# Two transformer blocks in one launch: TensorE's ticks crossed where two stages open, and norms, low parts and means of squares reordered in differential attention's last turns

## The reference

```python
for i in range(2):
    h = rms_norm(x, attn_norm[i])              # x * rsqrt(mean(x*x) + eps) * gain
    mix = stick_breaking_mixer(h, w_in[0], w_out[0]) if i == 0 else diff_mixer(h, ...)
    x = x + mix
    x = x + swiglu_ffn(rms_norm(x, ffn_norm[i]), w_gate[i], w_up[i], w_down[i])

# diff_mixer, 8 heads, two maps each:
a = softmax(q1 @ k1.T * scale, masked) - lam * softmax(q2 @ k2.T * scale, masked)
o = a @ v
o = rms_norm(o, sub_g) * (1 - lam_init)        # per head
return o @ w_out
# swiglu_ffn:
return (silu(h @ w_gate) * (h @ w_up)) @ w_down
```

## Time and profile before

| what | us |
|---|---|
| median of 3 runs | 2243.19 (2242.12 to 2243.57) |
| the profiled execution | 2241.81 |
| its span, first to last instruction | 2240.1 |
| TensorE busy in it | 2209.8 (99%) |
| VectorE, ScalarE, GpSimd busy | 1201.5, 935.8, 219.7 |

### The profile page before, as it was taken

One profiled execution on the slowest core, in us unless ns is written; L12 is line 12 of the kernel. 1 busy time (PEld: TensorE's weight loads), 2 busy tenths in 40 slices (PEclk: granted clock), 3 DMA queues, 4 the chain that ended last, 5 costly groups with the idle time before them and its releaser, 6 DMA issues.

```text
span 2240.1 us, 26887 instructions
## 1 busy us (share of the span) xinstructions
PE 2209.8 (99%) x10484; PEld 1727.7 (77%) x10484; DVE 1201.5 (54%) x1827; ACT 935.8 (42%) x1561; POOL 219.7 (10%) x312
## 2 busy tenths in 40 slices
PE   8999999999999999999999999999999999999999
PEld 6768888678888888877565888888886657888887
DVE  4574564564444444564444555554546685555454
ACT  4464334554432322334545433333335564333332
POOL 0000221211200000121323100000210001000000
PEclk9999999999999999999999999999999999999999
DMA  5212112114222232222111233322222112323233
GB/s 174 78 54 89 44 35 84 50 48 137 96 96 94 94 104 94 95 86 75 38 48 38 85 102 97 103 94 95 94 95 66 54 41 75 104 94 96 93 99 108
DMA packets 52110, 187.48 MB, mean 84 GB/s; under 512 B 5904, under 2 KB 6032, under 8 KB 51856
## 3 DMA queue, kind: packets, MB, share of 16 engines
q1 hardware_dynamic: 51984, 185.76, 25.4%
HBM read 183.64 MB, written 2.10 MB: 83 GB/s over the span
## 4 chain that ended last, share of the span: by engine, by line
PE 93%; DVE 3%; ACT 3%; issue 1%; DMA 0%; SPq 0%; ACTq 0%; DVEq 0%
PE ps L936 22%; PE ps L939 22%; PE ps L942 22%; PE ps L960 4%; PE ps L963 4%; PE ps L961 4%; PE ps L923 2%; PE ps L1283 2%; PE ps L1134 1%; PE ps L1167 1%; PE ps L1023 1%; PE ps L1271 1%; PE ps L1259 1%; PE ps L1287 1%; PE ps L1047 1%
## 5 line engine op out<-in xcount | busy, mean ns | idle before, releaser
L1335 ACT CAST wh<-raw 128x1024 fp32r<-128x1024 f32 (+1 forms) x336 | 352.9, 1050 | 869.6 <-PE ps L942 783.2
L1669 DVE TENSOR_TENSOR wl<-raw,wh 128x1024 fp32r<-128x1024 f32 (+1 forms) x336 | 416.4, 1239 | 175.5 <-ACT wh L1335 174.5
L936 PE MATMUL ps<-hh,wh 128*128 128x512 f32 x1408 | 450.9, 401 | 13.3 <-ACT hh L1351 11.9
L939 PE MATMUL ps<-hh,wl 128*128 128x512 f32 x1408 | 436.0, 391 | 0.4 <-DVE wl L1669 0.4
L942 PE MATMUL ps<-hl,wh 128*128 128x512 f32 x1408 | 435.2, 390 | 0.6 <-DVE hl L1748 0.6
L936 PEld LDWEIGHTS ps<-hh,wh 128*128 128x128 f32 x1408 | 258.7, 189 | 69.7 <-ACT wh L1335 10.2
L942 PEld LDWEIGHTS ps<-hl,wh 128*128 128x128 f32 x1408 | 264.8, 188 | 57.4 <-DVE hl L1748 1.0
L939 PEld LDWEIGHTS ps<-hh,wl 128*128 128x128 f32 x1408 | 264.5, 188 | 57.7 <-DVE wl L1669 1.8
L936 PE MATMUL ps<-R,wh 128*128 128x512 f32 x896 | 287.0, 401 | 0.0
L939 PE MATMUL ps<-R,wl 128*128 128x512 f32 x896 | 277.5, 390 | 2.4 <-DVE wl L1669 2.4
L942 PE MATMUL ps<-R,wh 128*128 128x512 f32 x896 | 276.7, 389 | 0.0
(11 more groups left out here) (225 smaller groups left out, 2193.1 us busy)
## 6 DMA issues: line engine op xcount, KB each, us to landing
raw<-in_weights SPq DMA_DIRECT2D x332, 512.0 KB, 3.3
x<-in_x_t SPq DMA_DIRECT2D x4, 512.0 KB, 7.1
F<-in_x_t SPq DMA_DIRECT2D x4, 512.0 KB, 4.4
out<-x SPq DMA_DIRECT2D x8, 256.0 KB, 2.0
raw<-in_weights SPq DMA_DIRECT2D x4, 416.0 KB, 3.2
x<-in_bias SPq DMA_DIRECT2D x1, 1024.0 KB, 6.4
C<-in_consts SPq DMA_DIRECT2D x1, 832.0 KB, 6.4
F<-in_weights SPq DMA_DIRECT2D x2, 384.0 KB, 3.6
```

Of the source, the lines that this page charges most:

```text
L936: pe.matmul(out, hi[:, k, cs], B.tile(u.src, k)[0], start=k == 0, stop=False)
L939: pe.matmul(out, lo[:, k, cs], B.tile(u.src, k)[0], start=False, stop=False)
L1335: act.copy(B.wh[s][:, 0:nk * ncol], B.raw[s][:, 0:nk * ncol]).then_inc(S["w_hi"], 1)
L1669: dve.tensor_tensor(lo, src, hi.bitcast(F32), ALU.subtract).then_inc(S[name], 1)
```

## The change

Five edits to the order, none to what is computed; the counts of instructions are the same on each engine, and the queues of GpSimd and SyncE are unchanged word for word.

1. `dense(..., crossed=True)` in two stages, the opening of the second block (`uq[0] + uk[0]`) and the last feed-forward (`ff2b`): the first two ticks of unit 1 stand before the last tick of unit 0.
2. `diff`, group 0: `df_norm` stands before `df_soft` of its tick (heads 0 and 1 of the group, where both fall together).
3. The low part of a head (L1970) is made one tick later, except the last head's.
4. In the last turn the led products come one step earlier among the attention's ticks.
5. In `lead`, what a tick issues is put in another order: the low part of a chunk and the evictions come before the deferred steps (`hl`, squares).

```diff
                     first = self.split(units[0].chunks[0] + 2)
-                    rest = first + rest + self.ready(u, j)
-                if not (b == u.nk and j == 0):
-                    rest += self.low()
+                    rest = first + self.ready(u, j) + (self.low() if j else []) + rest
+                else:
+                    rest = self.low() + rest
...
-    def dense(self, units, more=None):
+    def dense(self, units, more=None, crossed=False):
...
+            order += [(u, piece) for piece in pieces]
+        if crossed:
+            order = order[:3] + order[4:6] + order[3:4] + order[6:]
+        for u, piece in order:
+            self.place(u)
...
             yield ([("df_soft", d, n - 1)] if d.g and 1 <= n < 17 else []) + [("df", d, n)]
-            if d.g == 0 and n < 16:
-                yield [("df_soft", d, n)]
             h = d.since(n, 1)
             if h is not None:
                 yield [("df_norm", d, h)]
+            if d.g == 0 and n < 16:
+                yield [("df_soft", d, n)]
...
-        self.run(self.dense(uq[0] + uk[0], roots(2, True)))
+        self.run(self.dense(uq[0] + uk[0], roots(2, True), True))
...
-        self.run(tail[:1] + made[:1] + tail[1:3] + made[1:2] + tail[3:4] + made[2:3] + tail[4:5] + made[3:5] + tail[5:] + made[5:])
+        self.run(made[:1] + tail[:1] + made[1:2] + tail[1:3] + made[2:3] + tail[3:4] + made[3:4] + tail[4:5] + made[4:6] + tail[5:] + made[6:])
...
-        self.run(self.dense(chain(ff2b), roots(5)))
+        self.run(self.dense(chain(ff2b), roots(5), True))
...
-        h = d.since(n, 3)
+        h = 3 if n == 22 else d.since(n - 1, 3)
```

More of the change, by code:

```diff
@@ L339, in heads @@
         self.defer(5, "dn_root", u)
-    def dense(self, units, more=None):
-        n = 0
+    def dense(self, units, more=None, crossed=False):
+        n, order = 0, []
         for u in units:
-            self.place(u)
             if u.kind == "rows":
@@ L349, in dense @@
                 pieces = [(i, a, a + 2) for i in range(4) for a in range(0, 8, 2)]
[L350 to L364, removed]
+            order += [(u, piece) for piece in pieces]
[3 more added lines that the diff above has]
+            self.place(u)
+            tick, extra = self.low() + self.due(), (more or {}).get(n, [])
+            n += 1
+            if u.kind == "rows" and piece[2] % u.nk == 0:
+                steps = self.ready(u, piece[2] // u.nk - 1)
+                tick += steps[:-1] + extra + steps[-1:]
+            else:
+                tick += extra
+            if u.kind == "cols" and piece[2] == 8:
+                if piece[0] == 3:
+                    tick.append(("ev", u))
+                    if u.ev == "dq":
+                        self.heads(u)
+                tick += self.split(u.chunks[piece[0]] + 2)
+            yield [("mm", u, *piece)], tick
         rest = self.due(True)
```

## The result

| what | before | after |
|---|---|---|
| median, us | 2242.23 (2241.75 to 2244.27, 20 runs) | 2247.38 (2242.34 to 2249.22, 20 runs) |
| ratio of the times, 95% interval | | 1.0018 (1.0012 to 1.0025) |
| the profiled execution, its span | 2241.81, 2240.1 | 2244.68, 2242.9 |

A forecast was written before the change was run, and what follows sets the result against it. TensorE, busy 2209.8 of 2240.1 us, was taken as the bound, so only waits could change. Crossings 1.8 + 3.35 less gains 4.65 gave +0.5 on 2243.19: 2243.7 us, range 2240.0 to 2247.5.

The forecast's parts named there:

- The crossing at the opening: Where the second block opens: TensorE waits for unit 1's low weights, cost 1.8 us, between 1.5 and 2.2.
- The norm first: First head of differential attention: norm ahead of the exponentials removes TensorE's 0.88 us wait, gain 0.85 us, bounds 0 and 1.05.
- The low parts later: Differential attention: low part a tick later brings the maximum earlier, gain 1.3 us in the second group, 0.3 in the first.
- The last turn: Attention's last turn: earlier exponentials, and led products covering the 0.78 us wait for the logarithm, gain 1.75 us (0.7 to 2.4).
- the low weights ahead of `hl`: Output projection: VectorE makes low weights sooner, TensorE 1.9 us earlier there, but only 0.45 us kept (0 to 1.9).
- The crossing in the feed-forward: Last feed-forward: waits for unit 1's, then unit 2's low weights, cost 3.35 us, between 1.6 and 3.6.
- The sum: Whole kernel: crossings' costs 1.8 + 3.35 less gains of 4.65 make it +0.5 us.
- The rival that the clock falls in the longer stops: TensorE's clock halves after both crossings' stops, 2.4 us more each: 2248.5 us for both, 2246.1 for one; chance 0.09.
- The rival that the crossings are free: Both crossings cost nothing because something makes unit 1's low weights early; gains stand, 2238.5 us; chance 0.09.
- The rival that the gains are absorbed: TensorE meets the next wait; crossings cost 5.15 us, perhaps 1 of the gains is left: 2247.3 us; chance 0.10.

## Why the prediction was right or wrong

- *The crossing at the opening, +1.8.* Right in its mechanism and its size: 1.9 with the stop filled. But it was priced without the clock, which adds 1.5 to 2.7 in the three profiled executions with the full stop.
- *The norm first, -0.85.* The first wait went as counted (-0.92), but 0.3 came back by the next head, where I had found no wait and counted 0; alone it is worth 0.62.
- *The low parts later, -1.3 and -0.3.* Second group 1.22 (+0.32 to -0.90 in its ladder), first group 0.46 (+0.78 to +0.32). The 0.7 us that I had put down to the last turn because the exponentials come earlier belongs to this edit as well (0.76, from -0.90 to -1.66): 2.44 in all against 2.3.
- *The last turn and the low weights ahead of `hl`, what is left of -1.75 and -0.45.* 1.5 forecast, 1.2 measured. The ladder of the kernel after shows how what was won on the 2.40 of the earlier trace rows is lost again: 1.87 gained from the 269th to the 270th copy, 1.65 given back by the 272nd, as the sum had it.
- *The crossing in the feed-forward, +3.35.* 3.24 and 3.29 in the two ladders without a fall behind its stops. The price holds, the lengths of the stops less so: 1.37 and 1.88 were measured for the first, where 2.1 to 2.5 had been given.
- *The sum, +0.5.* Without a fall of the clock it would be 2243.2 - 2241.81 = +1.4 in time, of which 0.4 is the launch's chance: +1.0. The difference to 0.5 is that of the gains, 4.3 for 4.65.
- *The rival that the clock falls in the longer stops, 0.09.* This is what happened, and what failed in the forecast is that chance: the clock's falls were put at nothing in the sum. I had its place, about its price (2.4 a fall, measured 1.4 to 2.7) and nearly its outcome: 2248.5 for both, where the long executions take 2248.2 to 2249.2. That the outcome fits so well is in part luck: it stood on the base that was some 1 us too high, and the long execution that was profiled has three falls. I gave it little because the longest stop of the trace, the 2.40 of the earlier trace rows, had no slower pitch behind it. That was one execution. In six of the seven profiled executions that have this 2.40 us stop (the kernel before and the six experiments that keep it), the clock fell behind it; only that of the kernel before did not. The one execution on whose row I leaned was the exception; of the 101 timed executions of the kernel before only 15 have a mean granted clock of 1.000. Nor is it so that only the pitch can tell a fall: the page's slices do not show it, windows of 5 us do. At the kernel's own opening they do not, they read 1.00 at a pitch of 0.43.
- *The rival that the crossings are free* failed as argued, by VectorE's order; changing that order makes the one at the opening free and not the other. *The rival that the gains are absorbed* failed: of 4.65 us forecast 4.3 stand.

The Trainium skill (TensorE: Matmul & The Clock Gate, Why this matters for your kernels) advises against gaps without work between bursts of matmuls. The runs agree: the clock fell with a stop of 3.2 us in each of the three profiled executions that have it. They go further: it also fell behind stops of 1.8 to 2.4 us, in part of the executions.

## What to carry to other kernels

A unit that is moved forward to fill a wait must have its own inputs earlier than what it steps over: read on the queue of the engine that makes them what stands ahead, and move that first. Price a stop of some two or three microseconds of TensorE as its length plus a fall of the clock, 1.4 to 2.7 us here, unless a wait behind it takes the loss up; several shorter stops add risks that come and go from execution to execution. Where times spread with the granted clock, take a second profile and look at the clock in short windows around each stop before a stop is called harmless: the page's slices of 56 us show none of it.

## What the runs showed of the hardware that was not expected

- The clock falls in a given place in some executions and not in others, with the same instructions and the same stop. Behind 1.88 us in the feed-forward it fell in two of the three profiled executions with this stop (not in the first of the kernel after), behind 1.81 us in one of five. With 3.2 us it fell in three of three, but for different times: the pitch was 0.43 a matmul from 968.6 to about 972 in one, to about 973.7 in another.
- A fall needs no long stop. Around 1845, where TensorE stops three times (0.53, 0.57, 0.78) and does a few short matmuls between, it fell in three profiled executions (a cost of 1.5 to 1.6 us each) and not in three others with the same stops, the kernel before among them.
- A fall can be free. At 1865 to 1875 the windows read 0.81 and 0.84, and the ladder does not move by more than 0.02 us. Behind it the kernel before has a wait for ScalarE's `hh`, which takes the loss up: in the profiled executions with this fall and no crossing in the feed-forward, it is gone.

```profile
1879.58 0.50 PE L936 MATMUL ps<-hh,wh 128*128 128x512 f32 x1 [1.04 <-ACT hh L1351]
```

- VectorE's subtraction for the weights takes 1.21 us in one place and 1.70 in another, its `hl` 0.75 and 1.77. The longer ones lie beside GpSimd's additions; that these are the cause was not tried.
